# A gate projection of 768 products moved from a stage of its own into the differential attention stage

## What is computed

```
h = rms_norm(x, norm_mix)
proj = h @ w_in                        # 7 parts of 1024 columns
lru_in, lru_gate, q, k, v, g_lru, g_attn = split(proj)
y_lru  = (gelu(lru_gate) * rg_lru(conv(lru_in))) @ w_lru_o
o_attn = diff_attention(q, k, v, ...)  # 8 heads, two maps of 64 rows each, block-causal
y_attn = o_attn @ w_attn_o
mixed  = sigmoid(g_lru) * y_lru + sigmoid(g_attn) * y_attn
x = x + mixed @ w_out
x = x + memory_cross_attention(...);  x = x + hierarchical_moe(...)
```

## Time and profile before

| what | value |
|---|---|
| median of 3 runs | 4880.08 us (4880.0 to 4886.49) |
| profiled execution, its own time | 4875.11 us |
| span of its trace | 4873.3 us |
| PE busy | 4016.8 us (82%) |
| PEld busy | 3213.4 us (66%) |
| DVE busy | 2769.6 us (57%) |
| ACT busy | 2034.3 us (42%) |
| mean granted TensorE clock | 0.906 |

### The profile page before, as it was taken

How to read it: one execution, slowest core, us unless ns; L and a number is a source line. 1 busy time by engine, 2 the same in 40 slices (tenths; PEclk the granted TensorE clock), 3 DMA queues, 4 the chain that set the end, 5 groups by cost and what they waited for, 6 DMA issues and landing times. The chain is left out here.

```text
span 4873.3 us, 76497 instructions
## 1 busy us (share of the span) xinstructions
PE 4016.8 (82%) x31217; PEld 3213.4 (66%) x31217; DVE 2769.6 (57%) x4050; ACT 2034.3 (42%) x3437; POOL 470.9 (10%) x376
## 2 busy tenths in 40 slices
PE   6999877868887747999859888777779896499994
PEld 4888654448886526888748666665668655288883
DVE  4222154666654667999741675216652445399995
ACT  3111023645443315777531444116641333277772
POOL 0000012210001200111010231000000000111111
PEclk8999977979998878999969999889989898699997
DMA  5332212652223418999642333231112313699996
GB/s 198 130 135 95 105 64 63 188 149 78 80 75 126 142 71 356 389 398 390 260 160 86 99 110 103 95 118 40 40 57 82 112 52 128 252 402 411 412 412 250
DMA packets 368225, 842.35 MB, mean 173 GB/s; under 512 B 32207, under 2 KB 241135, under 8 KB 317446
## 3 DMA queue, kind: packets, MB, share of 16 engines
q1 hardware_dynamic: 349790, 787.43, 43.8%
q0 software_dynamic: 12032, 41.96, 2.7%
q10 hardware_dynamic: 6056, 8.08, 0.5%
HBM read 673.03 MB, written 164.35 MB: 172 GB/s over the span
## 5 line engine op out<-in xcount | busy, mean ns | idle before, releaser
L504 PE MATMUL psum<-proj_hi,proj_w 128*128 128x512 f32 (+2 forms) x1728 | 462.0, 356 | 15.4 <-DVE proj_w L546 13.8
L2719 DVE TENSOR_TENSOR moe_lo<-moe_raw,moe_hi 128x2048 fp32r<-128x2048 f32 x192 | 436.4, 2288 | 45.2 <-ACT moe_hi L2667 45.1
L4346 DVE TENSOR_TENSOR moe_lo<-moe_raw,moe_hi 128x2048 fp32r<-128x2048 f32 x192 | 428.2, 2284 | 33.7 <-ACT moe_hi L4301 33.7
L2667 ACT ACTIVATE moe_hi<-moe_raw 128x2048 fp32r<-128x2048 f32 x192 | 367.8, 1919 | 136.9 <-PE psum L2620 136.8
L4301 ACT ACTIVATE moe_hi<-moe_raw 128x2048 fp32r<-128x2048 f32 x192 | 356.9, 1910 | 41.5 <-PE psum L4262 41.5
L504 PEld LDWEIGHTS psum<-proj_hi,proj_w 128*128 128x128 f32 (+1 forms) x1728 | 304.1, 188 | 69.0 <-DVE proj_w L546 14.2
L504 PE MATMUL psum<-proj_lo,proj_w 128*128 128x512 f32 (+2 forms) x864 | 306.4, 355 | 0.0
L515 DVE COPY proj_out<-psum 128x512 f32<-128x512 f32 (+3 forms) x54 | 32.5, 602 | 355.3 <-PE psum L504 355.3
L1796 DVE COPY_PREDICATED chunks_X<-chunks_msk,psum 128x128 f32<-128x128 int32 x400 | 107.8, 301 | 161.5 <-PE psum L1549 137.3
L1709 ACT ACTIVATE chunks_T<-psum 128x128 f32<-128x128 f32 x400 | 103.1, 277 | 216.0 <-PE psum L1539 211.0
L504 PE MATMUL psum<-h_hi,proj_g_w 128*128 128x512 f32 x512 | 159.9, 394 | 29.2 <-DVE proj_g_w L546 29.2
(11 more groups left out here) (634 smaller groups left out, 9690.1 us busy)
## 6 DMA issues: line engine op xcount, KB each, us to landing
moe_raw<-in_w_down SPq DMA_DIRECT2D x128, 1024.0 KB, 8.1
moe_raw<-in_w_gate_up SPq DMA_DIRECT2D x128, 1024.0 KB, 10.3
moe_raw<-in_w_gate SPq DMA_DIRECT2D x64, 1024.0 KB, 9.0
moe_raw<-in_w_up SPq DMA_DIRECT2D x64, 1024.0 KB, 10.0
uT<-proj_out SPq DMA_DIRECT2D x35, 640.0 KB, 3.0
chunks_pr<-prim SPq DMA_DIRECT2D x40, 512.0 KB, 4.1
proj_raw<-in_w_in SPq DMA_DIRECT2D x17, 1024.0 KB, 7.8
hT<-in_w_mod SPq DMA_DIRECT2D x32, 512.0 KB, 4.7
```

The source lines that it names most:

```text
L504: ins = nc.tensor.matmul(bank[e * nch + c][0:width, 0:n], l, r, start=(k == 0 and i == 0), stop=(k == KD - 1 and i == 2))
L2667: nc.scalar.activation(hi[:, n % R], raw[:, n % RAW], ACT.Copy).then_inc(s["hi_ready"], 1)
L2719: nc.vector.tensor_tensor(lo[:, n % R], raw[:, n % RAW], hi[:, n % R], ALU.subtract).then_inc(s["lo_ready"], 1)
L4346: nc.vector.tensor_tensor(lo[:, n % R], raw[:, n % RAW], hi[:, n % R], ALU.subtract).then_inc(s["lo_ready"], 1)
```

## The change

The stage "proj_g" is gone. Its 768 products are made within `diff_attention`, as 32 units of 24 (one tile of 128 gate columns by 512 tokens, all of K), one unit with each of the 32 wide tiles: 12 products ahead of the transposes of the step, 12 behind them. They go to bank 7; the output transposes of each pair go to bank 5 instead, and since wide tiles use bank 5 they move to the narrow steps of the next odd head (GROUPS_AT from PAIR + 4 to PAIR + NT, NT = 8). ACT splits the gate weights, 128 columns at a time, and drains bank 7 after each unit; DVE takes the rest of the split. SP loads these weights and stores the gates.

`h_hi` and `h_lo` stay allocated until `route2` has ended. `mixed_T` uses them for the leading parts of its activations, `gemm_rows` for its split weights. The LRU branch is loaded at the start of `mixed_T`, in eight DMAs of 512 KB, and not at that of the attention stage; the block that issued it and its enclosing stage are gone.

```diff
@@ gemm_rows (and the same at its three uses of wt)
-        wt = st.sb("w", [P, 2, KK, D], F32R)
+        w_part = parts or (st.sb("w0", [P, KK, D], F32R), st.sb("w1", [P, KK, D], F32R))
@@ diff_attention
-        STATS, GROUPS_AT = PAIR + 2, PAIR + 4
+        STATS, GROUPS_AT = PAIR + 2, PAIR + NT
+        TILES_G = 2 * D // P
...
+        def unit_at(j):
+            return nb(j) if j < J and wide(j) else None
...
-                for h in range(2, HEADS2):
-                    sp.wait_ge(s["o_mm"], NT * (h - 1))
-                    load(h)
+                def load_g(c):
+                    if c >= TILES_G:
+                        return
+                    if c >= 2:
+                        sp.wait_ge(s["g_lo"], c - 1)
+                    sp.dma_start(g_raw[:, c % 2], x["w_in_2"][0][:, 5 * D + c * P:5 * D + (c + 1) * P].rearrange("(k p) n -> p k n", p=P))\
+                        .then_inc(g_in[c % 2], 16)
+
+                load_g(0)
+                load_g(1)
+                for u in range(2 * TILES_G):
+                    if u % 4 == 0 and 2 <= u // 4 + 1 < HEADS2:
+                        sp.wait_ge(s["o_mm"], NT * (u // 4))
+                        load(u // 4 + 1)
+                    if u % 2 == 0:
+                        load_g(u // 2 + 2)
+                    c, b = u // 2, u % 2
+                    sp.wait_ge(s["g_ev"], u + 1)
+                    sp.dma_start(gates[c * P:(c + 1) * P, b * BANK:(b + 1) * BANK], g_out[:, u % 4, :]).then_inc(g_stored[u % 4], 16)
...
@@ PE
+                    if wide(j) and j > GROUPS_AT:
+                        pe.wait_ge(s["out"], 4 * ((j - GROUPS_AT) // PAIR + 1))
...
+                    pe.wait_ge(s["evB"], min(nb(PAIR * p + GROUPS_AT), nb(J)))
                     for t in range(4):
-                        ins = nc.tensor.transpose(bank[7][:, t * P:(t + 1) * P], o[:, (PAIR * p + 4 * g + t) % SLOTS_O, :], ident)
+                        ins = nc.tensor.transpose(bank[5][:, t * P:(t + 1) * P], o[:, (PAIR * p + 4 * g + t) % SLOTS_O, :], ident)
...
+                def gate_unit(u, part):
+                    c, b = u // 2, u % 2
+                    if part == 0:
+                        pe.wait_ge(s["g_lo"], c + 1)
+                        if u:
+                            pe.wait_ge(s["g_ev"], u)
+                    for k in range(4 * part, 4 * part + 4):
+                        for i, (l, r) in enumerate(((0, 0), (1, 0), (0, 1))):
+                            ins = nc.tensor.matmul(bank[7][:, :], g_w[:, c % 2, l, k, :], h_part[r][:, k, b * BANK:(b + 1) * BANK],
+                                                   start=(k == 0 and i == 0), stop=(k == KD - 1 and i == 2))
+                    if part == 1:
+                        ins.then_inc(s["g_mm"], 1)
...
+                    u = unit_at(j)
+                    if u is not None:
+                        gate_unit(u, 0)
                     if 1 <= j <= J:
                         turn(j - 1)
+                    if u is not None:
+                        gate_unit(u, 1)
@@ ACT
+                def gate_leading(c):
+                    act.wait_ge(g_in[c % 2], 16 * (c // 2 + 1))
+                    if c >= 2:
+                        act.wait_ge(s["g_mm"], 2 * (c - 1))
+                    nc.scalar.activation(g_w[:, c % 2, 0, :, :], g_raw[:, c % 2], ACT.Copy).then_inc(s["g_hi"], 1)
+
+                def gate_out(u):
+                    act.wait_ge(s["g_mm"], u + 1)
+                    if u >= 4:
+                        act.wait_ge(g_stored[u % 4], 16 * (u // 4))
+                    nc.scalar.activation(g_out[:, u % 4, :], bank[7][:, :], ACT.Copy).then_inc(s["g_ev"], 1)
+
+                gate_leading(0)
                 act.wait_ge(s["lam"], 1)
...
+                    if u is not None:
+                        gate_out(u)
+                        if u % 2 == 0 and u // 2 + 1 < TILES_G:
+                            gate_leading(u // 2 + 1)
@@ DVE
+                def gate_rest(c):
+                    dve.wait_ge(s["g_hi"], c + 1)
+                    nc.vector.tensor_tensor(g_w[:, c % 2, 1, :, :], g_raw[:, c % 2], g_w[:, c % 2, 0, :, :], ALU.subtract)\
+                        .then_inc(s["g_lo"], 1)
...
+                gate_rest(0)
                 for j in range(STEPS):
...
+                    u = unit_at(j - 1) if j else None
+                    if u is not None and u % 2 == 0 and u // 2 + 1 < TILES_G:
+                        gate_rest(u // 2 + 1)
@@ mixed_T
-                load(1)
+                for k in range(KD):
+                    sp.dma_start(act_T[0][:, k, :], lru[k * P:(k + 1) * P, :]).then_inc(lru_in[k], 16)
+                    if k == 3:
+                        load(1)
...
+                    if n == 0:
+                        act.wait_ge(lru_in[k], 16)
@@ second
-        gemm_T(nc, bank, "proj_g", None, T, x["w_in_2"][0], 5 * D, (D // P, ()), uT2[5 * D:7 * D, :], split=(h_hi, h_lo))
```

More of the change, by code:

```diff
@@ L2091, in rwkv, with gemm_rows @@
             rwkv_combine(nc, bank, cst, tabs, y, bonus, gate, lT)
-def gemm_rows(nc, bank, name, cst, actT, K, w, x, out, hT, grow=None, exchanged=(), h_col=None, h_rows=None, h_out=None):
+def gemm_rows(nc, bank, name, cst, actT, K, w, x, out, hT, grow=None, exchanged=(), h_col=None, h_rows=None, h_out=None, parts=None):
     KK = K // P
@@ L3205, in _, with diff_attention @@
                         turned(n - 2)
-def diff_attention(nc, psum, bank, cst, col, x, qkT, v_rows, oT):
+def diff_attention(nc, psum, bank, cst, col, x, qkT, v_rows, oT, h_part, g_w, g_raw, g_out, gates):
     J = HEADS2 * NT
@@ L3266, in _ @@
                 load(1)
-                for h in range(2, HEADS2):
-                    sp.wait_ge(s["o_mm"], NT * (h - 1))
-                    load(h)
+                def load_g(c):
[16 more added lines that the diff above has]
+                    sp.dma_start(gates[c * P:(c + 1) * P, b * BANK:(b + 1) * BANK], g_out[:, u % 4, :]).then_inc(g_stored[u % 4], 16)
+                for i in range(4):
+                    sp.wait_ge(g_stored[i], 16 * (TILES_G // 2))
             @block.gpsimd
@@ L3461, in _, with mixed_T @@
                         scale(*pair_at(j, STATS + 1, 2))
-def mixed_T(nc, bank, w_a, w_b, act_T, act_lo, a_in, gates, mT):
+                    u = unit_at(j - 1) if j else None
+                    if u is not None and u % 2 == 0 and u // 2 + 1 < TILES_G:
+                        gate_rest(u // 2 + 1)
+def mixed_T(nc, bank, w_a, w_b, lru, act_T, act_lo, act_hi, gates, mT):
     RAW, R = 2, 3
@@ L3471, in mixed_T @@
         w_hi, w_lo = st.sb("w_hi", [P, R, KD, P], F32R), st.sb("w_lo", [P, R, KD, P], F32R)
-        act_hi = st.sb("act_hi", [P, 2, KD, T], F32R)
+        lru_in = [st.sem(f"lru_in{k}") for k in range(KD)]
         g = st.sb("g", [P, 2, T])
@@ L3546, in _ @@
                 leading(0)
-                act.wait_ge(a_in, 16)
                 for n in range(2):
@@ L4487, in second @@
     gT, qkT, v_rows = scratch("gT", D, T), scratch("qkT", 2, D, T), scratch("v_rows", T, D)
-    with nc.sbuf_tensor("h_hi", [P, KD, T], F32R) as h_hi, nc.sbuf_tensor("h_lo", [P, KD, T], F32R) as h_lo:
-        add_norm_split(nc, bank, cst, x1, acc, gate_row, x["norm_mix_2"], x2, h_hi, h_lo)
-        gemm_T(nc, bank, "proj_lru", None, T, x["w_in_2"][0], 0, (D // P, ()), uT2[0:2 * D, :], split=(h_hi, h_lo))
-        qkv_and_lru(nc, bank, cst, col, x, h_hi, h_lo, uT2, gT, qkT, v_rows)
-        gemm_T(nc, bank, "proj_g", None, T, x["w_in_2"][0], 5 * D, (D // P, ()), uT2[5 * D:7 * D, :], split=(h_hi, h_lo))
     if stop == "heads":
@@ new lines, in second @@
+        with nc.sbuf_tensor("h_hi", [P, KD, T], F32R) as h_hi, nc.sbuf_tensor("h_lo", [P, KD, T], F32R) as h_lo:
+            add_norm_split(nc, bank, cst, x1, acc, gate_row, x["norm_mix_2"], x2, h_hi, h_lo)
+            gemm_T(nc, bank, "proj_lru", None, T, x["w_in_2"][0], 0, (D // P, ()), uT2[0:2 * D, :], split=(h_hi, h_lo))
+            qkv_and_lru(nc, bank, cst, col, x, h_hi, h_lo, uT2, gT, qkT, v_rows)
+            with nc.sbuf_tensor("g_w", [P, 2, 2, KD, P], F32R) as g_w, nc.sbuf_tensor("g_raw", [P, 2, KD, P], F32) as g_raw,\
+                    nc.sbuf_tensor("g_out", [P, 4, BANK], F32) as g_out:
+                pass
+            with nc.sbuf_tensor("mT", [P, KD, T], F32) as mT:
+                with nc.sbuf_tensor("attn_raw", [P, KD, T], F32) as attn:
+                    pass
+                with nc.sbuf_tensor("attn_rest", [P, KD, T], F32R) as attn_rest:
+                    diff_attention(nc, psum, bank, cst, col, x, qkT, v_rows, attn, (h_hi, h_lo), g_w, g_raw, g_out, uT2[5 * D:7 * D, :])
+                    with nc.sbuf_tensor("lru_raw", [P, KD, T], F32) as lru:
+                        pass
+                    with nc.sbuf_tensor("lru_rest", [P, KD, T], F32R) as lru_rest:
+                        mixed_T(nc, bank, x["w_lru_o_2"][0], x["w_attn_o_2"][0], gT, (lru, attn), (lru_rest, attn_rest), (h_hi, h_lo),
+                                uT2[5 * D:7 * D, :], mT)
```

(18 more changed lines are left out.)

45 lines of the change are left out of this document (11 added, 34 removed).

## The result

| | kernel before | changed kernel |
|---|---|---|
| median | 4880.04 us (4867.44 to 4886.49) | 4796.81 us (4795.96 to 4808.89) |
| profiled execution, span | 4873.3 us | 4807.0 us |
| PE busy | 4016.8 us | 4007.2 us |
| mean granted TensorE clock | 0.906 | 0.906 |

The ratio is 0.9847, 95% interval 0.9819 to 0.9874: faster by 1.3 to 1.8%. In two more sets of runs the changed kernel gave 0.9875 (0.9855 to 0.9896) and 0.9866 (0.9839 to 0.9892). The forecast was 4810 us, the range 4790 to 4836 us. The medians differ by 83, 64 and 66 us in the three sets. The spans of the two profiled executions differ by 66.3 us.

The account below looks back on a forecast made before the run. PE was taken to bound "proj_g", a ring of scores, maxima and exponentials the attention stage. Terms -192 + 129 - 11 + 7.5 - 4 + 1 - 1 = -70 us gave 4805, forecast 4810 us; range 4796 to 4826, with two rivals 4790 to 4836.

Parts of the forecast that it names:

- wide parts: Attention stage, steps of tiles 4 to 7: gate products and lower clock bring eight heads to 301 us, +129 us.
- narrow parts: gained: Narrow step 0: full clock in heads 1, 2, 4, 6 gives -5 us, no wait for weights about -2 us.
- narrow parts: output transposes: Narrow steps of heads 3, 5, 7: moved output transposes and ACT's copy cost 2.5 us a head, +7.5 us.
- behind the wide parts, to the last copy: End of the attention stage: last tile's transposes no longer wait for weights and run at a higher clock, -4 us.
- start of the attention stage: First maxima 16 us after the first DMA, with less data to land first, -4 us (between -7 and 0).
- start of `mixed_T`: First activations now come behind the first weights, and the others at the load rate: +1 us (0 to 4).
- the clock rival: Units run at the lower clock level: all of them cost 153 us more, 4963 us; chance 0.02.
- The bound changes: Wide steps: the ring of scores, maxima and exponentials bounds them before, PE after; 1.6 us free in tile 5's step.
- The ring kept no idle time: Rival, wide steps: ring stays and the unit is added to it, nothing hidden, +51 us, 4861 us; chance 0.04.
- bank 7 held nobody up: Rival, wide steps: PE waits 0.5 to 1 us a step on bank 7, 4826 to 4842 us; chance 0.10.
- The clock stays up: Rival: dense wide steps carry the full clock through the narrow ones, -14.7 us, 4795 us; chance 0.06.
- 0.190 us: Rival, gate units: products start closer together than 0.227 us, 28 us less, 4782 us; chance 0.01.

Follow-up runs that it names:

- the runs with 12, 6 and 2 products: Changed kernel with only 12, 6 or 2 of each unit's 24 products, the rest left out: medians 4710.08, 4678.42 and 4671.20 us.
- the run with one start a step: Changed kernel with both halves of a unit behind the turning (the step's transposes), none ahead: median 4794.91 us, ratio 0.9858 to the kernel before.
- the run with the split moved: Changed kernel with the first gate weights' split moved from the stage's head to steps 2 and 3 of head 0: 4801.21 us, repeated 4794.22 us.
- the products in step 3: Changed kernel with halves of units also in narrow step 3 of heads 1 to 7: median 4772.08 us, ratio 0.9805 to the kernel before.

## Why the prediction was right

Each term of the sum against what the two traces show:

| term | forecast, us | measured, us |
|---|---|---|
| stage "proj_g" gone | -192.0 | -192.0 |
| wide parts | +129 | 300.4 - 171.7 = +128.7 |
| narrow parts: gained | -7 | -10.5 |
| narrow parts: output transposes | +7.5 | +3.9 |
| behind the wide parts, to the last copy | -4 | -3.7 |
| start of the attention stage | -4 | -0.9 |
| between stages | -1 | +0.2 |
| start of `mixed_T` | +1 | +0.7 |

Without the last row they sum to -74.3 us, with it to -73.6, 3 us beyond the forecast of the trace. The median of 4796.81 us lies 13 us under the 4810 forecast, and the other two sets have 4804.64 and 4801.98 for the same kernel; the part of the 13 us that no term shows can't be told from the scatter of the rest of the program. (The last wide part of the kernel before is taken to its last exponential, that of the changed kernel to the transposes of the last tile, which wait for nothing there.)

Three small slips stand in the working and move nothing: the four steps sum to 13.6 us, not 13.7, the terms to -70.5, and all cases but the clock rival and the last make 0.97, not 0.96.

**The bound changes.** This was the main step and it holds: PE is busy in every part of every wide step, and the runs with 12, 6 and 2 products show both sides of the kink. The free time of a step had been read as 1.6 us from one step; the kink is at 6 to 7 products, 1.4 to 1.5 us, and over 32 steps 174 - 128.7 = 45 us were hidden, 1.4 each.

**The size of the wide term** is right by two errors that cancel. PE's work in a head at full clock was taken as 35.5 us and is 36.3. For the difference, 8 x 0.8 = 6.7 us in all, the sum had 2 us for changes between kinds of products. A head has eight starts of gate products, two a wide step, and the timeline shows 0.1 us more at each (0.56 against 0.46 us), which makes the 0.8 us; the run with one start a step gives 0.09 us for the one left out. The lower clock was taken as 14.7 us and is 0.04 x 37.75 + 0.08 x (39.06 + 39.16 + 39.15) = 10.9 us by the granted clocks, or 9.8 us by how much longer these four parts are than head 1's. That it was kept from the kernel before was right for heads 0, 2, 4 and 6 and wrong for heads 3, 5 and 7: their wide parts now run at 1.00, where all had been given head 0's 0.94.

**The narrow parts.** Both terms were mis-sized. In heads 1, 2, 4 and 6 the gain is 2.0 to 2.1 us each where 1.3 + 0.3 stood, and heads 3, 5 and 7 gain 0.7 to 0.9 each besides the transposes. Head 1 with 6 products a unit shows the two parts: its narrow part is 12.12 us at a clock of 1.00, so 1.3 of the 2.0 us are the clock, as forecast, and the remaining 0.65 are the wait for weights in step 0, for which 0.3 stood. For the output transposes I had priced ACT's copy as if it stood in the ring. The steps of head 3 are 4.27, 3.50 and 5.01 us, the last over steps 2 and 3, against 3.84, 3.06 and 4.57 in head 1. Each grew by 0.43 to 0.44 us, as long as four transposes on PE, and nothing is left over for the copy. Steps 2 and 3 hold two groups of four, and one of them is hidden: PE waits 1.33 us for weights in step 3 of head 3, 1.76 in head 1. That makes 1.3 us a head for 2.5 forecast, and the narrow parts of heads 3, 5 and 7 came out about 0.5 us longer than before, not 2 to 3. Moving the transposes by themselves wasn't tried.

**The start** is the step that failed. "3 to 4 us of splits and small steps follow" took the landing of the data as 11 to 12 us. It was 15.0 us: the first gate weights are the eleventh load in SP's queue, issued 4.8 us after the first, and the second ones, which the term didn't count, are issued right behind them. Behind the landing came 4.3 us of splits, table load and small steps. The term also took the loads as the bound; the run with the split moved shows that the order on ACT and DVE was.

**The rivals.** The ring kept no idle time, bank 7 held nobody up, and the clock fell no further. "The clock stays up" was half true, in heads 3, 5 and 7. Products cost the same in the units as in "proj_g" (0.227 us): two wide steps that differ by 12 products differ by 2.75 us, 0.229 each. So neither 0.190 us nor the 131 ns of the Trainium skill, page "TensorE: Matmul & The Clock Gate", section "Back-to-back issue gap", is seen here.

The load of 4 MB that moved from the attention stage to `mixed_T` was not undone by itself. Its new place costs 0.7 us ahead of the first product of `mixed_T` (8.2 us after the first DMA, 7.6 before).

## What to carry to other kernels

Work put on an engine that idles is free only up to the idle time of the step it stands in, and from there on costs its full length; so put it where the waits are longest, which here also kept the clock up in the step behind. Work that stands ahead of a loop, on an engine of the loop's ring, delays the ring until its data land: give it a place inside the loop, ahead of its first use. And where stages with the same code start up to 17 us apart from one trace to the next, judge an edit of a few us by the stretch of its own stage.

## What the runs showed that was not expected

- Taking idle time out of narrow step 3 took the lower clock out of the wide step behind it. Head 2's wide part had a clock of 0.92 behind 4.3 us of waits and 1.00 behind none. Heads 4 and 6 read the same. Waits ahead are not the whole story, though: with the split moved, head 1's clock fell to 0.96 behind the same narrow steps that had 1.00 behind them in the changed kernel. With the products in step 3 the whole part of head 2 stands at 1.00 (3198.83:3229.66 above); in the changed kernel its first 6.1 us are these:

```profile
3209.22:3215.35 6.13, 6.13 (x21) 4.27 (x21) 4.33 (x9) 2.60 (x8) 0.00 (x0) 0.52 0.12 29
```

- Each start of a run of gate products among other kinds costs about 0.1 us on PE in a stretch where it never idles: its first pair takes 0.56 us, the others 0.46 us.
- With 6 and 2 products the narrow step 0 of head 1 is 4.48 us, with 12 and 24 it is 3.84: PE waits for `attn_w` in 16 places there and in 8 or 9 with 12 and 24, so the wait for weights in step 0 goes only where PE, not the ring, sets the steps ahead of it.
